# First mLSTM layer of a two-layer decoder step: values with tokens on partitions, stabiliser rows spread by DMA, sample queries in four column groups

## The chip, the cores and the metric

One core of one Trainium2 chip runs the whole program. The metric is the device time of one execution in microseconds. The kernel before took 1507.76 us, the median of three runs (1506.08 to 1508.02). The execution that the profiler recorded took 1506.18 us; its trace spans 1504.4 us, and all times "at" below are microseconds from the start of that span.

## The reference

A prompt of 512 tokens and 8 single-token samples, 520 columns in all, pass through two layers of width 1024. Each layer is a token mixer, a gated MLP with a width-3 causal convolution (inner width 2816), and a per-layer embedding term. Layer 0 mixes with an mLSTM (4 heads, keys of 128, values of 256), layer 1 with sliding-window attention. The change touches layer 0's mixer alone. Written for one head over the whole prompt (zero initial state, so that the chunked form of the reference comes to one causal product):

```
b = cumsum(log_sigmoid(f));   m_t = b_t + max(0, max_{s<=t}(i_s - b_s))
p[s,t]  = (k_s . q_t) / sqrt(128) * exp(b_t - b_s + i_s - m_t)      for s <= t
num_t   = sum_s p[s,t] v_s;   qn_t = sum_s p[s,t]
h_t     = num_t / max(|qn_t|, exp(-m_t));   y = (sigmoid(o) * h) @ w_out
C_new   = sum_s w_s k_s v_s^T;   n_new = sum_s w_s k_s              (the prompt's final state)
```

Each sample updates its own stored memory, C = w_old C + w_new k v^T (4 heads of 128x256), reads it with its query, and gets h in the same way. C, n and m of prompt and samples are outputs too.

## The kernel before

Everything is float32. Features lie on partitions and tokens on the free axis: `h`, `xH`, `xL` are [128, 8, 520]. A projection runs as three rounded products (high by high, low by high, high by low), in chunks of 128 output features. For each chunk SP loads 512 KB of weights into a slot of a three-slot ring, or for some chunks one of five extra slots (`load`, L380); ACT rounds them to `wH` (`high`, L486); DVE subtracts to get `wL` (`low`, L1275); PE multiplies (L798 to L802, in `mout` L808 to L810, where each half of 260 tokens is a unit of its own); and DVE reads the result out of PSUM, scaled (L1315). Each engine's order is the order in which it is written; semaphores alone tie the engines together. PSUM has four tiles of two banks: `tile[0]`, `tile[1]`, `sums`, `side`.

Layer 0's mixer goes through these stages:

- `kv` (13 chunks): gates, keys, values. In its first chunk DVE makes the rows `brow` (cumulated log forget gate), `mrow` (running maximum) and the samples' rows; the last sets `s_rows` (L1383). `erow` is exp(-m).
- Turning: PE transposes keys and values to tokens-on-partitions (`ktok`, `vtok`, L880, L882) and turns small rows to columns (L887 to L893): `acol` holds the exponent per key token.
- `qo` (12 chunks: 4 of queries, 8 of the output gate). Behind each of the last 8 chunks stands one sample's outer product (`sample_products`, L915) and the query of the sample before (`memory_query`, L903): four matmuls, one for each head, 8 columns of stationary `qmask` and 256 moving columns of the memory. All four write partitions 0 to 7 of `sums`, side by side on the free axis. The memories go through a two-buffer ring that POOL loads and stores.
- Behind `qo`: the last query, the samples' normaliser product (L929), a copy `stok` of the queries' results (8 x 1024, L1463), eight small transposes (L933), and the samples' output (L1466 to L1479).
- Four heads. `spread_scores(n)` spreads `mrow` to 128 partitions with a 4-row matmul into `sums[:, 0]` (L942), then makes the four causal blocks of scores (L949) in `tile`. DVE adds the causal mask (`diag`, L1488, into `cg`), ACT makes the decays in `prob` (7 exponentials, L580 and L583), DVE multiplies scores in (`weights`, L1502). `values(n)` multiplies with the values as stationary, features out, up to 512 tokens moving (L964, into both banks of `side`), a column sum by a one-hot stationary of 4 columns (L966, into `tile[1][0:4, 1]`), and the final memory (L974) with its normaliser (L977, one moving column) into `sums[:, 1]`. DVE multiplies by the gate (L1526), copies the final memory (L1529), and weighs the next head's keys (`final_weights`, L1513, into `kw`).
- Behind all heads: DVE makes one over the denominators of all heads on 4 partitions (L1535 to L1538), PE spreads it by four 4-row matmuls (L992), DVE multiplies (L1549), ACT rounds to `xH` (L589), DVE makes `xL` (L1543).
- `mout` (8 chunks, 16 units), whose first unit waits for `xL` row block by row block. Loads 3 to 7 use extra slots that lie over the mixer's tensors and so wait for them (L372 to L380).

## Time and profile before

| | us |
|---|---|
| median of three runs | 1507.76 |
| the profiled execution, its own time | 1506.18 |
| its span | 1504.4 |
| PE busy (matmul) | 1431.6 |
| DVE busy | 880.7 |
| ACT busy | 571.2 |

The profile is one execution. "PEclk" in it is the clock that TensorE was granted as a share of full speed: 1.00 is the 2.4 GHz level, 0.50 the 1.2 GHz level. A PE row counts records; a float32 matmul leaves two of them, a float32 transpose one. In a timeline row the first number is where the group starts and the second how long until its last result is out; consecutive PE rows overlap, so the pace is read from the starts. In the chain of waits a piece's length is the time that it alone held the end back.

### The profile page before, as it was taken

To read this page: it belongs to the slowest core of one execution; us is meant where nothing else is said; L and a number is where in the kernel's file an instruction comes from. 1 tells how busy PE (TensorE), PEld (TensorE's weight loads), DVE (VectorE), ACT (ScalarE), POOL (GpSimd) and SP (SyncE) were. 2 spreads that over 40 slices of the span, in tenths; PEclk is the share of its full clock that TensorE was granted. 3 is DMA by queue.
4 is the path that set the end of the run, shared out by engine and by line. 5 is a ranking of instruction groups with operands and counts; after the bars stand their busy time and mean duration, and the time that the engine had idled before them with its cause. 6 is when DMAs were issued, how large, how long until landed. Compare 5 with 4: busy or idle time off the path is not lost.

```text
span 1504.4 us, 25607 instructions
## 1 busy us (share of the span) xinstructions
PE 1431.6 (95%) x11049; PEld 1352.4 (90%) x11049; DVE 880.7 (59%) x1571; ACT 571.2 (38%) x1001; POOL 32.3 (2%) x55
## 2 busy tenths in 40 slices
PE   6999989899999999999999978899999999999987
PEld 6989855699999999999889966699999999999977
DVE  4435553658777777322766565757877777522464
ACT  5121131355444444222543124655444444322452
POOL 2000100000000000000100010000000000000000
PEclk9999999899999999999999987999999999999999
DMA  7222530221223233322323230022223233322222
GB/s 224 73 83 71 185 124 0 71 85 43 76 94 94 90 96 104 117 80 90 127 71 93 76 90 1 1 88 68 71 87 97 87 96 92 124 97 86 72 57 100
DMA packets 33442, 130.86 MB, mean 87 GB/s; under 512 B 4057, under 2 KB 4145, under 8 KB 32929
## 3 DMA queue, kind: packets, MB, share of 16 engines
q1 hardware_dynamic: 28368, 110.36, 23.3%
q0 software_dynamic: 4960, 18.86, 4.0%
q8 instruction: 87, 1.43, 0.4%
q14 instruction: 27, 0.21, 0.0%
HBM read 120.57 MB, written 10.04 MB: 87 GB/s over the span
## 4 chain that ended last, share of the span: by engine, by line
PE 86%; DVE 9%; ACT 3%; issue 1%; DMA 1%; SPq 0%; POOL 0%; DVEq 0%; ACTq 0%
PE tile L798 21%; PE tile L800 21%; PE tile L802 21%; PE tile L808 3%; PE tile L809 3%; PE tile L810 3%; PE side L964 1%; PE side L1195 1%; PE sums L839 1%; DVE wL L1275 1%; DVE sm L1799 1%; DVE soft L1814 1%; ACT wH L486 1%; PE sums L903 1%; PE tile L966 1%
## 5 line engine op out<-in xcount | busy, mean ns | idle before, releaser
L486 ACT ACTIVATE wH<-raw 128x1024 fp32r<-128x1024 f32 (+1 forms) x193 | 214.3, 1111 | 487.0 <-DMA raw<-in_w_up 147.5
L798 PE MATMUL tile<-xH,wH 128*128 128x260 f32 x1872 | 381.3, 285 | 17.2 <-DVE xL L1347 11.1
L802 PE MATMUL tile<-xH,wL 128*128 128x260 f32 x1872 | 378.7, 284 | 0.0
L800 PE MATMUL tile<-xL,wH 128*128 128x260 f32 x1872 | 378.4, 284 | 0.0
L1275 DVE TENSOR_TENSOR wL<-raw,wH 128x1024 fp32r<-128x1024 f32 (+1 forms) x193 | 249.2, 1291 | 183.9 <-ACT wH L486 179.6
L798 PEld LDWEIGHTS tile<-xH,wH 128*128 128x128 f32 x1872 | 290.7, 190 | 21.2 <-issue 20.4
L802 PEld LDWEIGHTS tile<-xH,wL 128*128 128x128 f32 x1872 | 290.2, 189 | 0.0
L800 PEld LDWEIGHTS tile<-xL,wH 128*128 128x128 f32 x1872 | 289.7, 189 | 0.0
L1315 DVE TENSOR_TENSOR u<-tile,rstd 128x520 f32<-128x520 f32 x102 | 71.3, 699 | 155.1 <-PE tile L802 155.1
L798 PE MATMUL tile<-hidH,wH 128*128 128x260 f32 x616 | 124.3, 283 | 0.0
L802 PE MATMUL tile<-hidH,wL 128*128 128x260 f32 x616 | 123.8, 282 | 0.0
L800 PE MATMUL tile<-hidL,wH 128*128 128x260 f32 x616 | 123.8, 282 | 0.0
L808 PE MATMUL tile<-xH,wH 128*128 128x260 f32 x384 | 117.5, 306 | 3.3 <-DVE wL L1275 3.0
L809 PE MATMUL tile<-xL,wH 128*128 128x260 f32 x384 | 111.4, 290 | 0.0
L810 PE MATMUL tile<-xH,wL 128*128 128x260 f32 x384 | 111.2, 289 | 0.0
L800 PEld LDWEIGHTS tile<-hidL,wH 128*128 128x128 f32 x616 | 95.1, 188 | 0.0
L802 PEld LDWEIGHTS tile<-hidH,wL 128*128 128x128 f32 x616 | 94.9, 188 | 0.0
L798 PEld LDWEIGHTS tile<-hidH,wH 128*128 128x128 f32 x616 | 94.8, 188 | 0.0
L808 PEld LDWEIGHTS tile<-xH,wH 128*128 128x128 f32 x384 | 75.2, 196 | 7.3 <-DVE wL L1275 3.8
L809 PEld LDWEIGHTS tile<-xL,wH 128*128 128x128 f32 x384 | 75.2, 196 | 0.8
L810 PEld LDWEIGHTS tile<-xH,wL 128*128 128x128 f32 x384 | 75.2, 196 | 0.0
L1315 DVE TENSOR_TENSOR kvq<-tile,rstd 128x520 f32<-128x520 f32 x24 | 16.8, 698 | 81.6 <-PE tile L802 81.6
(297 smaller groups left out, 1983.3 us busy)
## 6 DMA issues: line engine op xcount, KB each, us to landing
raw<-in_w_up SPq DMA_DIRECT2D x88, 512.0 KB, 3.6
raw<-in_w_down SPq DMA_DIRECT2D x32, 704.0 KB, 4.1
raw<-in_w_ple SPq DMA_DIRECT2D x16, 512.0 KB, 3.6
raw<-in_w_kv SPq DMA_DIRECT2D x13, 512.0 KB, 3.7
raw<-in_w_qo SPq DMA_DIRECT2D x12, 512.0 KB, 3.6
raw<-in_w_qkv SPq DMA_DIRECT2D x12, 512.0 KB, 3.7
cring<-in_c_in POOLq DMA_DIRECT2D x8, 512.0 KB, 3.9
out_c_s<-cring POOLq DMA_DIRECT2D x8, 512.0 KB, 3.5
```

Of the source, the lines that this page charges most:

```text
L486: nc.scalar.activation(wH[j][:, 0:n], raw[j][:, 0:n], ACT.Copy).then_inc(s_high, 1)
L798: nc.tensor.matmul(out[:, q, 0:HT], wh, x[0][:, k, tokens(q)], start=first, stop=False)
L800: nc.tensor.matmul(out[:, q, 0:HT], wh, x[1][:, k, tokens(q)], start=False, stop=False)
L802: mm = nc.tensor.matmul(out[:, q, 0:HT], wl, x[0][:, k, tokens(q)], start=False, stop=last)
L808: nc.tensor.matmul(out, wh, x[0][:, k, tokens(q)], start=first, stop=False)
L809: nc.tensor.matmul(out, wh, x[1][:, k, tokens(q)], start=False, stop=False)
L810: return nc.tensor.matmul(out, wl, x[0][:, k, tokens(q)], start=False, stop=last)
L839: nc.tensor.matmul(sums[:, q, 0:HT], ones, sq[:, k % 2, tokens(q)], start=(k == 0), stop=(k == KT - 1)).then_inc(s_squ, 1)
L903: mm = nc.tensor.matmul(sums[0:DEC, n // 2, (n % 2) * DV:(n % 2 + 1) * DV], qmask[:, b % 2, n, :], cring[:, b % 2, n, :], start=b == 0 and ...
L964: nc.tensor.matmul(side[:, half, j * P:SEQ], vtok[:, j, n, half * P:half * P + P], pj, start=(j == 0), stop=(j == NB - 1), skip_group_chec ...
L1275: nc.vector.tensor_tensor(wL[j][:, 0:n], raw[j][:, 0:n], wH[j][:, 0:n].bitcast(F32), ALU.subtract).then_inc(s_low, 1)
L1315: nc.vector.tensor_tensor(halves(dst), bank(stage, c)[0:rows, :, 0:HT], halves(rstd[0:rows, :]), ALU.mult).then_inc(s_read, 1)
```

## The change

- Values: the stationary operand is now a 128x128 block of `prob` and the moving one the values with a 257th column of ones, so numerator and denominator come out together, tokens on partitions. For each head there are four accumulation groups (blocks 3, 2, 1, 0 with 4, 3, 2, 1 matmuls) and a fifth for the final memory (4 matmuls). The five groups go through three PSUM banks in turn.
- DVE makes one over each block's denominator (three instructions on one column, `denominators`), ACT copies the block scaled by it to `ytok` (`numerators`), PE transposes eight blocks per head back (`turn_numerators`), and DVE multiplies by the gate (`gated`). Rounding for `mout` (`x_high`, `o_low`) follows head by head. The stages behind all heads (L1535 to L1538, L992, L1549) go.
- `mrow` is stored to DRAM and read back by four DMAs, each to all 128 partitions; they are on POOL's queue, ahead of the samples' memories. The spreading matmuls (L942) go. `diag` and the decays of heads 0 and 1 are made during `qo`.
- `exp(-m)` becomes a column too: four more small matmuls and one small copy.
- A sample query's four matmuls write four partition groups, 0, 32, 64 and 96, of one bank. `stok` becomes 104 x 256, turned by two transposes.
- Order: `scores(0)` stands ahead of the last query, `scores(1)` behind the sample turns; `weights(0)` ahead of the samples' output; `low("mout", 2)` within head 1.
- `mout` loads 3 to 7 get other extra slots and other waits.

```diff
+            pool.wait_ge(s_rows, 1)
+            pool.dma_start(g.m_rows, mrow[:]).then_inc(s_mst, 16)
+            pool.wait_ge(s_mst, 16)
+            pool.wait_ge(s_squ, KT)
+            for n in range(NH):
+                pool.dma_start(mspread[n], g.m_rows[n:n + 1, :].to_broadcast([P, SEQ])).then_inc(s_mspread, 16)
...
@@ mout loads
                 if stage == "mout" and k == NRING:
-                    sp.wait_ge(s_snum, DEC)
+                    sp.wait_ge(s_st_t, 1)
                 if stage == "mout" and k == NRING + 1:
-                    sp.wait_ge(s_num, NH)
                     for b in range(2):
                         sp.wait_ge(s_cst[b], 16 * DEC // 2)
                 if stage == "mout" and k == NRING + 2:
+                    sp.wait_ge(s_num, NB * NH)
+                if stage == "mout" and k == NRING + 3:
                     sp.wait_ge(s_cps, 16)
+                if stage == "mout" and k == NRING + 4:
                     sp.wait_ge(s_afin, NH + 1)
+                    sp.wait_ge(s_out, 16 * 4)
...
@@ ACT
+            def numerators(n):
+                for i, b in enumerate(reversed(range(NB))):
+                    e = (NB + 1) * n + i
+                    act.wait_ge(s_num, NB * n + i + 1)
+                    act.wait_ge(s_den, NB * n + i + 1)
+                    nc.scalar.activation(ytok[:, b, :], num_bank(e)[:, 0:DV], ACT.Copy,
+                                         scale=rden[:, (NB * n + i) % (2 * NB):(NB * n + i) % (2 * NB) + 1]
+                                         ).then_inc(s_nr, 1)
...
             for c in range(COUNT["qo"]):
                 high(*ahead("qo", c + 2))
+                if c in (1, 5):
+                    decays(c // 4)
...
+            for n in range(NH):
+                numerators(n)
+                if n + 2 < NH:
+                    decays(n + 2)
+                x_high(n)
...
@@ PE
+                nc.tensor.matmul(sums[:, 1, 160 + NH * b:160 + NH * b + NH], erow[:, b * P:b * P + P],
+                                 ident[0:NH, 0:NH], start=True, stop=True)
...
@@ memory_query
-                    mm = nc.tensor.matmul(sums[0:DEC, n // 2, (n % 2) * DV:(n % 2 + 1) * DV], qmask[:, b % 2, n, :],
-                                          cring[:, b % 2, n, :], start=b == 0 and n % 2 == 0, stop=b == DEC - 1,
+                    mm = nc.tensor.matmul(sums[32 * n:32 * n + DEC, 0, 0:DV], qmask[:, b % 2, n, :],
+                                          cring[:, b % 2, n, :], start=b == 0, stop=b == DEC - 1,
                                           skip_group_check=True)
...
+            def num_bank_free(e):
+                n, i = divmod(e - 3, NB + 1)
+                if e == 2:
+                    pe.wait_ge(s_qnr, 1)
+                if e >= 3 and i == NB:
+                    pe.wait_ge(s_cfr, n + 1)
+                elif e >= 3:
+                    pe.wait_ge(s_nr, NB * n + i + 1)
+
             def values(n):
                 pe.wait_ge(s_prob, n + 1)
...
+                for i, b in enumerate(reversed(range(NB))):
+                    e = (NB + 1) * n + i
+                    num_bank_free(e)
+                    for j in range(b + 1):
+                        at0 = starts[j] + (b - j) * P
+                        mm = nc.tensor.matmul(num_bank(e)[:, 0:DV + 1], prob[:, n % 2, at0:at0 + P], vtok[:, j, n, :],
+                                              start=(j == 0), stop=(j == b))
+                    mm.then_inc(s_num, 1)
+                e = (NB + 1) * n + NB
+                num_bank_free(e)
+                pe.wait_ge(s_kw, n + 1)
                 for j in range(NB):
...
+                    mm = nc.tensor.matmul(num_bank(e)[:, 0:DV + 1], kw[:, j, :], vtok[:, j, n, :], start=(j == 0),
+                                          stop=(j == NB - 1))
                 mm.then_inc(s_cf, 1)
+            def turn_numerators(n):
+                pe.wait_ge(s_nr, NB * (n + 1))
+                pe.wait_ge(s_afin, n + 1)
+                for half in range(2):
+                    for b in range(NB):
+                        mm = nc.tensor.transpose(turned_num(half)[:, b * P:b * P + P],
+                                                 ytok[:, b, half * P:half * P + P], ident)
+                mm.then_inc(s_numt, 1)
+            scores(0)
+            memory_query(DEC - 1)
...
+            scores(1)
             for n in range(NH):
                 values(n)
                 if n + 2 < NH:
-                    spread_scores(n + 2)
+                    scores(n + 2)
+                turn_numerators(n)
...
@@ DVE
+            def denominators(n):
+                for i, b in enumerate(reversed(range(NB))):
+                    dve.wait_ge(s_num, NB * n + i + 1)
+                    r = rden[:, (NB * n + i) % (2 * NB):(NB * n + i) % (2 * NB) + 1]
+                    total = num_bank((NB + 1) * n + i)[:, DV:DV + 1]
+                    chain.link(nc.vector.scalar_tensor_tensor(out=r, in0=total, scalar=-1.0, in1=ecol[:, b, n:n + 1],
+                                                              op0=ALU.mult, op1=ALU.max))
+                    chain.link(nc.vector.tensor_tensor(r, total, r, ALU.max))
+                    nc.vector.reciprocal(r, r).then_inc(s_den, 1)
...
             for c in range(COUNT["qo"]):
                 scaled_read("qo", c, kvq[:, c + 3 * NH if c < NH else c, :])
                 low(*ahead("qo", c + 2))
+                if c in (0, 4):
+                    diag(c // 4)
                 if c >= NH:
                     new_memory(c - NH)
...
             for n in range(NH):
                 if n + 1 < NH:
                     weights(n + 1)
+                if n:
+                    o_low(n - 1)
+                denominators(n)
+                last_memory(n)
                 if n + 1 < NH:
                     final_weights(n + 1)
                 if n + 2 < NH:
                     diag(n + 2)
+                if n == 1:
+                    low("mout", 2)
+                gated(n)
             clear_acc()
+            o_low(NH - 1)
```

## Rows read from the trace of the kernel before

**Rows 1.** The page: shares of the span in the chain that ended last.
```profile
PE 86%; DVE 9%; ACT 3%; issue 1%; DMA 1%; SPq 0%; POOL 0%; DVEq 0%; ACTq 0%
```
**Rows 2.** Windows: stretch, length, busy us (records) by engine, PEclk, DMA share, GB/s.
```profile
204.00:223.00 19.00, 13.92 (x45) 7.01 (x44) 10.49 (x26) 10.45 (x18) 1.59 (x3) 0.84 0.26 83
223.00:271.00 48.00, 47.99 (x180) 24.79 (x179) 14.65 (x28) 4.72 (x14) 0.00 (x0) 0.99 0.04 9
271.00:289.00 18.00, 12.54 (x32) 7.31 (x33) 15.75 (x18) 5.61 (x9) 0.65 (x2) 0.62 0.19 68
```
**Rows 3.** Chain of waits around the heads: start, us, what held the end.
```profile
213.96 1.28 ACT L580
...
272.79 3.35 DVE mrow L1538
```
**Rows 4.** PE timeline of the heads and of `mout`'s second unit: start, us, what.
```profile
222.75 2.46 PE L964 MATMUL side<-prob,vtok 128*128 128x512 f32 x4
...
234.62 2.42 PE L949 MATMUL tile<-kvq 128*128 128x512 f32 x8
...
248.17 2.42 PE L949 MATMUL tile<-kvq 128*128 128x512 f32 x8
...
270.04 0.95 PE L977 MATMUL sums<-const,cv 128*128 128x1 f32 x8
...
289.10 0.28 PE L808 MATMUL tile<-xH,wH 128*128 128x260 f32 x1
```
**Rows 5.** PE timeline of one sample query, one of seven behind `qo` chunks.
```profile
195.10 1.89 PE L903 MATMUL sums<-cring,qmask 128*8 128x256 f32 x8
196.93 0.51 PE L798 MATMUL tile<-xH,wH 128*128 128x260 f32 x2
```
**Rows 6.** Layer 1: matmuls of two column halves on PE, and the clock there.
```profile
900.17 1.12 PE L1218 MATMUL sums<-softT,vst 128*64 128x128 f32 x8
...
900.10:901.25 1.15, 1.15 (x10) 0.75 (x9) 0.91 (x4) 0.38 (x1) 0.00 (x0) 0.50 0.80 175
```
**Rows 7.** PE timeline of the turning stage: transposes and rows made columns.
```profile
103.31 0.60 PE L882 MATMUL side<-const,kvq 128*128 128x128 f32 x4
103.75 0.27 PE L880 MATMUL sums<-const,kvq 128*8 128x128 f32 x1
...
113.58 1.05 PE L887 MATMUL sums<-const,cv 4*128 4x4 f32 x8
```
**Rows 8.** DVE timeline: the operations that the new order uses.
```profile
204.98 1.65 DVE L1442 SCALAR_TENSOR_TENSOR cring<-cring,sbc,side 128x256 f32<-128x256 f32 x4
...
211.84 0.19 DVE L1469 TENSOR_TENSOR rs<-rs,sbc 128x32 f32<-128x32 f32 x1
212.07 0.35 DVE L1470 RECIPROCAL rs<-rs 128x32 f32<-128x32 f32 x1
...
237.89 1.68 DVE L1502 SCALAR_TENSOR_TENSOR prob<-tile,prob 128x512 f32<-128x512 f32 x4 [2.48 <-ACT prob L580]
244.52 1.29 DVE L1526 TENSOR_TENSOR kvq<-side,kvq 128x512 f32<-128x512 f32 x2 [4.94 <-PE tile L966]
...
283.49 1.30 DVE L1543 TENSOR_TENSOR xL<-kvq,xH 128x520 fp32r<-128x520 f32 x2
```
**Rows 9.** ACT timeline: a copy out of PSUM, and two roundings to `xH`.
```profile
283.60 1.17 ACT L589 ACTIVATE xH<-kvq 128x520 fp32r<-128x520 f32 x2 [1.19 <-DVE kvq L1549]
...
289.30 0.39 ACT L528 ACTIVATE y_ml<-tile 128x260 f32<-128x260 f32 x1 [1.23 <-PE tile L810]
```
**Rows 10.** DVE timeline in `kv`: a chunk's `wL`, and the end of the chunk before.
```profile
62.82 1.23 DVE L1275 TENSOR_TENSOR wL<-raw,wH 128x1024 fp32r<-128x1024 f32 x1
67.85 0.70 DVE L1315 TENSOR_TENSOR kvq<-tile,rstd 128x520 f32<-128x520 f32 x1 [3.81 <-PE tile L802]
```
**Rows 11.** Windows of layer 1's attention: columns as in rows 2.
```profile
900.00:920.00 20.00, 15.20 (x85) 11.68 (x83) 8.73 (x29) 6.87 (x25) 0.00 (x0) 0.67 0.07 21
...
940.00:960.00 20.00, 17.51 (x138) 12.81 (x136) 14.70 (x43) 12.58 (x48) 0.00 (x0) 1.00 0.00 1
```

More of the change, by code:

```diff
@@ L100 @@
 STACK = 64 + DEC
+STOK = 32 * (NH - 1) + DEC
 class Chain:
@@ L475, in o_tile, with num_bank, turned_num @@
             return kvq[:, NH + k, :]
+        def num_bank(e):
+            return (tile[1][:, 1, :], side[:, 0, :], sums[:, 1, :])[e % 3]
+        def turned_num(half):
+            return (side[:, 1, :], sums[:, 0, :])[half]
         @block.scalar
@@ L959, in values @@
-                at0 = 0
-                for j in range(NB):
-                    w = SEQ - j * P
-                    pj = prob[:, n % 2, at0:at0 + w]
-                    for half in range(2):
-                        nc.tensor.matmul(side[:, half, j * P:SEQ], vtok[:, j, n, half * P:half * P + P], pj,
-                                         start=(j == 0), stop=(j == NB - 1), skip_group_check=True)
-                    mm = nc.tensor.matmul(tile[1][0:NH, 1, j * P:SEQ], hot[:, n, :], pj, start=(n == 0 and j == 0),
-                                          stop=(n == NH - 1 and j == NB - 1), skip_group_check=True)
-                    at0 += w
@@ L979, in values @@
-                mm.then_inc(s_cf, 1)
-            spread_scores(0)
-            spread_scores(1)
+                starts = [j * SEQ - j * (j - 1) // 2 * P for j in range(NB)]
+                for i, b in enumerate(reversed(range(NB))):
[6 more added lines that the diff above has]
+                    mm.then_inc(s_num, 1)
@@ new lines, in _ @@
+            scores(0)
+            memory_query(DEC - 1)
+            pe.wait_ge(s_prod, 1)
+            nc.tensor.matmul(sums[:, 1, 0:NH * DEC], ones, ntmp[:, 0].rearrange("p n b -> p (n b)"),
+                             start=True, stop=True).then_inc(s_qns, 1)
+            pe.wait_ge(s_stok, 1)
+            for half in range(2):
+                mm = nc.tensor.transpose(side[:, 1, half * P:half * P + STOK], stok[:, half * P:half * P + P],
+                                         ident[0:STOK, 0:STOK])
@@ new lines, in last_memory, with gated, o_low @@
+            def last_memory(n):
+                dve.wait_ge(s_cf, n + 1)
+                nc.vector.tensor_copy(cfin[:, n, :], num_bank((NB + 1) * n + NB)[:, 0:DV + 1]).then_inc(s_cfr, 1)
+            def gated(n):
+                dve.wait_ge(s_numt, n + 1)
+                for half in range(2):
+                    o = kvq[:, NH + 2 * n + half, 0:SEQ]
+                    last = nc.vector.tensor_tensor(o, turned_num(half), o, ALU.mult)
+                last.then_inc(s_afin, 1)
+            def o_low(n):
+                for k in (2 * n, 2 * n + 1):
+                    dve.wait_ge(s_xh, XSET["mout"] + k + 1)
+                    nc.vector.tensor_tensor(xL[:, k, :], o_tile(k), xH[:, k, :].bitcast(F32), ALU.subtract
+                                            ).then_inc(s_xr, 1)
@@ new lines, in _ @@
+            mask(0)
+            for c in range(COUNT["qo"]):
+                scaled_read("qo", c, kvq[:, c + 3 * NH if c < NH else c, :])
+                low(*ahead("qo", c + 2))
+                if c in (0, 4):
+                    diag(c // 4)
+                if c >= NH:
+                    new_memory(c - NH)
+            wold, wnew = sbc[:, :, 0, :], sbc[:, :, 1, :]
+            chain.did(nc.vector.tensor_tensor(nst[:], nst[:], wold, ALU.mult))
+            chain.link(nc.vector.tensor_tensor(ntmp[:, 0], kvq[:, 0:NH, SEQ:T], wnew, ALU.mult))
@@ new lines, in _ @@
+            dve.wait_ge(s_qnr, 1)
+            chain.link(nc.vector.scalar_tensor_tensor(out=flat_rs, in0=flat_rs, scalar=-1.0, in1=flat_rs,
+                                                      op0=ALU.mult, op1=ALU.max))
+            chain.link(nc.vector.tensor_tensor(rs[:], rs[:], sbc[:, :, 2, :], ALU.max))
+            chain.link(nc.vector.reciprocal(rs[:], rs[:]))
+            dve.wait_ge(s_st_t, 1)
+            for half in range(2):
+                chain.did(nc.vector.tensor_tensor(
+                    stmp[:, :, half, :],
+                    side[:, 1, half * P:half * P + P].rearrange("p (n x) -> p n x", n=NH)[:, :, 0:DEC],
+                    rs[:], ALU.mult))
```

191 lines of the change are left out of this document (63 added, 128 removed).

## The prediction

> **What bounds the kernel now.** I read first the shares of the chain of waits: PE holds 86% of the span and DVE 9% [rows 1], so time is won where PE does less or stands still less. Then the windows around the mixer's core [rows 2]. Three stretches differ. From 204 to 223 PE is busy 13.9 of 19 us at a granted clock of 0.84. From 223 to 271, the four heads, it is busy without a gap at 0.99, while DVE works 15 and ACT 5 of 48 us. From 271 to 289 it is busy 12.5 of 18 us at 0.62. So the heads are bound by PE's own work and the two ends by short serial steps on other engines, with a clock that falls to its 1.2 GHz level behind them. The chain shows such steps: 1.28 us of ACT ahead of the first exponential (its table) and 3.35 us of DVE for one reciprocal over 512 columns on 4 partitions [rows 3]. One head with scores behind it takes 248.17 - 234.62 = 13.55 us; the heads last from 222.75 to 270.99, 48.2 us, and `mout`'s second unit starts at 289.10, 18.1 us later [rows 4].
>
> **Part 1, rows made columns: +1.0 us.** Four more matmuls like L887, which took 1.05 us for four [rows 7], in a stretch where PE runs without waiting. Their DVE copy lies in DVE's idle time.
>
> **Part 2, queries in four column groups: -7.1 us ahead of the last memory.** A query takes 196.93 - 195.10 = 1.83 us of PE [rows 5], about 0.22 for each of eight records. Nothing of before runs four groups of 32 columns; the nearest is layer 1's L1218, whose outputs lie in two halves of 64 partitions. Eight records of 128 columns took at most 1.12 us at a clock of 0.50 [rows 6]. One after the other they would take 8 x 0.22 = 1.76 us: transposes of 128 columns come every (103.75 - 103.31)/4 = 0.11 us at full clock [rows 7], so 0.22 at half. Two halves do run side by side. For four groups the best is 2 records in sequence, 0.45 us, the worst the 1.83 of now, or 0.1 more if each group has an entry of its own. I take 0.65, near the best, since two halves came close to halving. That saves 1.2 us for each of the six queries that stand wholly before the last sample's update; the other two are counted in part 3.
>
> The Trainium skill, "TensorE: Matmul & The Clock Gate", Part 3 (packing small matmuls), has three column tiles 2.38 times as fast as one by one. By that a query would cost 1.83/2.38 = 0.77 us, an estimate, and the part would save 0.7 us less. The rows on two halves show side-by-side work, not how far four go.
>
> **Part 3, from the last memory to the first values: -10.5 us.** Before, DVE ends the last memory at 204.98 + 1.65 = 206.6 [rows 8] and values start at 222.75 [rows 4]: 16.1 us, in which the samples' output, spreading, mask, table load, exponentials and scores stand in line. In the new order masks and decays of heads 0 and 1 are made during `qo` and `scores(0)` runs while DVE updates the last memory. Left is: last query 0.65; DVE's four small operations, begun with the query, end at 0.8 (0.2 each); `weights(0)` 1.6 [rows 8] to 2.4; `stok` 0.4 (256 columns against 0.65 for 512, L1526) to 2.8; PE's two transposes and the hop 0.4; `scores(1)` 2.4 [rows 4] to 5.6. The samples' output lies beside `scores(1)`. 16.1 - 5.6 = 10.5. The masks in `qo` add 0.7 us to DVE and the decays 2.4 us to ACT (DVE's wait between mask and weights, L1502 in rows 8), in chunks of 5.8 us or more where both idle; without that cover the sum of 3 us would come back for each head.
>
> **Part 4, four heads: 48.2 to 38 us, -10.2.** PE's work is 14 matmuls of 257 columns at 1.83/4 = 0.46 [rows 5], 6.4 us; scores 2.4 for the first two heads; eight transposes at 0.11, 0.9 with their entry. That is 9.6 or 7.3 us, if nothing waits. But PE's fourth group needs the bank of the first, and the fifth that of the second; each bank is freed by three DVE steps and an ACT copy. The nearest rows for the DVE steps are 0.19 (whose successor starts 0.23 later) and 0.35 for a reciprocal of 32 columns [rows 8]; I take 0.55 for three on one column, with 0.9 as the upper bound and 0.4 as the lower, and 0.4 for the copy (0.39, L528) [rows 9]. Counted from the first values:
> - Head 0: DVE is free in time. 9.6.
> - Head 1: mask 2 ends at about 8.2, ACT loads its table (1.3) [rows 3] and makes decays (2.4): 11.9. `weights(2)` 1.6, `o_low` 1.3 (L1543) [rows 8], one turnover 0.95: 15.8. PE could have started the fourth group at 13.7: 2.1 us lost. End 21.3.
> - Head 2: `gated(1)` 1.3 (L1526), `weights(3)` 1.6, `o_low` 1.3, turnover 0.95 with hops: 26.6; the fourth group could start at 25.4: 1.2 lost. No scores. End 29.8.
> - Head 3: no `weights`; about 0.3 lost. End 37.4; with hops between engines 38.
> `low("mout", 2)` (1.23) lies in head 1 while PE makes scores and transposes. The two DVE operations and the copy of the final memory that stand before the mask, at most 0.65 each, fit beside the scores.
>
> **Part 5, behind the heads: 18.1 to 3.8 us, -14.3.** One over all denominators, its spreading and four multiplications are gone, and `xL` for heads 0 to 2 is ready. PE goes straight into the first unit with six of eight row blocks. The last two wait for `gated(3)` 1.4, ACT's two roundings 1.17 [rows 9], the second `o_low` 0.65, and one block of products 0.4: 3.7, or 3.8 with hops. The moved loads have cover: load 5 now waits for the last numerators, 6 for the stored memory, 7 for `gated(3)`, and with some 2.9 us for a unit their chunks come later than 4 us of landing and 2.3 of rounding.
>
> **Part 6, spreading by DMA: 0.** 1 MB into SBUF around 45 to 60 us, beside weight loads. A chunk's `wL` was done at 64.05 and needed at 67.85 [rows 10]: 3.8 us of slack. Bounds 0 and +3 (a load held up by twice its slack, once). Nothing on POOL's queue is due before the first memory is stored, some 90 us later.
>
> **The clock: +4.** The new heads stall at 1 to 2 us, three times, and the start has two idle stretches near 2 us. Layer 1's attention has such alternation: 0.67 granted while PE was busy 15.2 of 20 us, but 1.00 at 17.5 of 20 [rows 11]. I price 8 us of PE work at the 1.2 GHz level, which adds 4; the bounds are 0 and about 9 (all 32 us of PE work in the heads at 0.7, less the stalls that this fills).
>
> **Sum.** 1.0 - 7.1 - 10.5 - 10.2 - 14.3 + 4 = -37.1 us. The profiled execution took 1506.18 (span 1504.4), so 1469.1; the median is 1.6 above it: 1470.7, which I put at 1470.5.
>
> **The rivals.**
> - *The clock falls through the heads.* Waits for freed banks break PE's work up as in layer 1's slow stretch [rows 11], against it stands its fast stretch with much the same work. Price: +9 instead of +4, 1475.5. The Trainium skill, "TensorE: Matmul & The Clock Gate", "A second HAM failure mode: psum-queue depth-cycling", says that going round PSUM banks can make small idles after which the clock swings between its levels. By that rule this is the case that comes; layer 1 shows both.
> - *The column groups don't run side by side.* Then the part does nothing of what it says: 8 x 1.2 = 9.4 back, 1480. For it: no row has 32-column groups; against it L1218 [rows 6].
> - *The turnover of banks is dearer.* 0.9 for DVE's three steps holds the fourth and fifth group back by 0.35 each in three heads, 2.1 us; with the DMA's 3 us, 1475.6.
> - *Slower than before.* The clock stays at 1.2 GHz from the start of the heads on. Each microsecond of PE work at full clock costs one more; stalls absorb 4. It decides at 41 + 4 = 45 us of such work: all of the heads (32) and the first five of `mout`'s 16 units. If all units ran so: 32 - 4 + 46 = 74 more than the 1466.5 without a clock term, 1541. Against it: behind the stall before `mout` the clock came back within the first unit, at 289 [rows 4], and PE has no wait behind it.
>
> **How the numbers follow.** Forecast 0.66 (its own range 1463 to 1475), clock 0.13, columns 0.10, turnover 0.06, slower 0.04, no change 0.01. The time is the forecast's, 1470.5. Downwards the range takes in no clock loss (-4), a query at 0.45 (-1.6) and cheaper hops: 1461. Upwards it takes in the columns' case with half a clock term more: 1484. About 0.2% (3 us) is what can be told from no change. Faster 0.95, same 0.01, slower 0.04.
>
> **What would show it.** In the profile after: a query near 0.65 us of PE with record starts close together; first values 5 to 6 us behind the last memory; the heads 38 us long with PE waiting for ACT's `ytok` copies ahead of each fourth group, most in head 1; L1535 to L1549 gone and `mout`'s second unit within 4 us of the last transposes; no longer idle time of ACT on loads from 45 to 65 us. I am wrong if the heads take over 45 us, if a query stays at 1.8 us, or if PE waits for DVE at the first mask.

## The result, and the profile after

| | before | after |
|---|---|---|
| median, us | 1507.50 (1506.08 to 1508.02, 4 runs) | 1465.34 (1459.84 to 1466.75, 4 runs) |
| profiled execution, its own time | 1506.18 | 1466.03 |
| its span | 1504.4 | 1464.2 |
| PE busy / DVE busy / ACT busy | 1431.6 / 880.7 / 571.2 | 1395.0 / 876.8 / 579.0 |

The ratio is 0.9718, with a 95% interval of 0.9701 to 0.9736: 42.2 us less between the medians, 40.2 between the spans. The point was 1470.5, so it lay 5 us too high; the time is inside the range of 1461 to 1484.

The first view is the chain of waits of the kernel after, by engine. It answers to [rows 1].

```profile
PE 85%; DVE 10%; ACT 2%; issue 2%; DMA 1%; SPq 0%; POOL 0%; DVEq 0%; ACTq 0%
```

The shares hardly move, since 1300 of the 1460 us are the same work. The windows say more. These three of the kernel after run from the last memory to the first values, over the four heads, and to `mout`'s second unit. They answer to [rows 2], with the columns of those.

```profile
199.30:205.40 6.10, 4.46 (x21) 2.71 (x22) 4.49 (x18) 1.85 (x2) 1.59 (x3) 0.83 0.54 171
205.40:242.30 36.90, 33.70 (x162) 27.24 (x161) 24.90 (x82) 17.10 (x37) 0.00 (x0) 0.98 0.08 26
242.30:246.40 4.10, 3.47 (x28) 3.08 (x26) 3.46 (x6) 2.11 (x3) 0.55 (x1) 1.00 0.42 163
```

Before, the same three took 16.1, 48.2 and 18.1 us [rows 2, 4]. PE is now busy 33.7 of the heads' 36.9 us, where it was busy all of 48, and DVE and ACT carry 24.9 and 17.1 instead of 15 and 5. The granted clock over the heads is 0.98.

The PE timeline of the kernel after shows the heads; it answers to [rows 4]. A row is start, length, line, operands, records, and the idle time in front.

```profile
161.30 0.62 PE L945 MATMUL sums<-cring,qmask 128*8 128x256 f32 x8
...
202.21 3.37 PE L980 MATMUL tile<-kvq 128*128 128x512 f32 x8
205.37 2.59 PE L1002 MATMUL tile<-vtok,prob 128*128 128x257 f32 x8
...
215.34 1.90 PE L1002 MATMUL sums<-vtok,prob 128*128 128x257 f32 x8
...
220.72 0.70 PE L1002 MATMUL sums<-vtok,prob 128*128 128x257 f32 x2 [1.31 <-ACT ytok L606]
...
226.03 1.90 PE L1002 MATMUL side<-vtok,prob 128*128 128x257 f32 x8
...
231.40 0.70 PE L1002 MATMUL side<-vtok,prob 128*128 128x257 f32 x2 [1.31 <-ACT ytok L606]
...
234.56 1.90 PE L1002 MATMUL tile<-vtok,prob 128*128 128x257 f32 x8
...
239.20 0.70 PE L1002 MATMUL tile<-vtok,prob 128*128 128x257 f32 x2 [0.58 <-ACT ytok L606]
...
242.28 0.37 PE L848 MATMUL tile<-xH,wH 128*128 128x260 f32 x1
...
245.31 0.39 PE L848 MATMUL tile<-xH,wH 128*128 128x260 f32 x1 [0.63 <-DVE xL L1552]
...
246.38 0.28 PE L848 MATMUL tile<-xH,wH 128*128 128x260 f32 x1
```

The four rows of eight records (205.37, 215.34, 226.03, 234.56) are the first groups of the heads, so the heads take 9.97, 10.69, 8.53 and 7.72 us. The rows of two records with an idle time are each head's fourth group, waiting for the copy that frees the first group's bank. The chain of waits through head 1 (start, us, what held the end) tells why that copy is late:

```profile
215.57 0.57 issue
216.15 0.68 DVE kvq L1546
216.83 1.59 DVE prob L1514 x4
218.42 1.22 DVE xL L1552 x2
219.74 0.17 DVE rden L1535
219.93 0.17 DVE rden L1536
220.19 0.48 ACT ytok L606
220.72 0.70 PE sums L1002 x2
```

DVE makes the second half of `gated(0)`, `weights(2)` and `o_low(0)`, 3.5 us of the path in a line, before it comes to the denominator for which ACT and then PE wait. `weights(2)` and `o_low(0)` are the sequence that part 4 of the forecast named; `gated(0)` it had off the path in head 1.

**The ledger.** All times are read from the two PE timelines and the DVE timelines.

| step | forecast | measured | from |
|---|---|---|---|
| 1, rows made columns | +1.0 | +0.9 | from start to start: eight matmuls in 1.88 us, 113.23 to 115.11, where four took 0.98 before, 113.58 to 114.56 |
| 2, six queries | -7.1 | -7.8 | 1.30 less for each, by e1 to e3 |
| 3, last memory to first values | -10.5 | -10.1 | 6.04 for 16.1 |
| 4, heads | -10.2 | -11.3 | 36.9 for 48.2 |
| 5, behind the heads | -14.3 | -14.0 | 4.1 for 18.1 |
| 6, DMA | 0 | 0 | chunks of `kv` every 5.77 us in both |
| clock | +4 | within 3 and 4, and behind the mixer | below |

The sum to `mout`'s second unit is 289.10 - 246.38 = 42.7 us less; the parts give 42.3. From there to the end the code is the same, and it took 1215.3 us before and 1217.8 after: 2.5 us go back.

### The profile page after: what moved, and what is told of

Read it like the earlier page. It is cut to its first block, busy times and chain, and to the rows that moved or that the text cites. A ratio compares the mean times of both kernels' runs of the same rounds, so it can differ in the third digit from the quotient of the medians.

```text
span 1464.2 us, 25626 instructions
## 1 busy us (share of the span) xinstructions
PE 1395.0 (95%) x11019; PEld 1345.6 (92%) x11019; DVE 876.8 (60%) x1613; ACT 579.0 (40%) x1017; POOL 35.3 (2%) x61
## 4 chain that ended last, share of the span: by engine, by line
PE 85%; DVE 10%; ACT 2%; issue 2%; DMA 1%; SPq 0%; POOL 0%; DVEq 0%; ACTq 0%
PE tile L838 22%; PE tile L842 22%; PE tile L840 22%; PE tile L848 3%; PE tile L849 3%; PE tile L850 3%; PE side L1241 1%; PE sums L879 1%; DVE sm L1852 1%; DVE wL L1321 1%; DVE soft L1867 1%; DVE cv L1346 1%; ACT wH L507 1%; PE side L848 1%; PE side L850 1%
## 5 line engine op out<-in xcount | busy, mean ns | idle before, releaser
L838 PE MATMUL tile<-xH,wH 128*128 128x260 f32 x1872 | 380.9, 285 | 16.7 <-DVE xL L1393 10.4
```

What stands on the lines that cost most here:

```text
L838: nc.tensor.matmul(out[:, q, 0:HT], wh, x[0][:, k, tokens(q)], start=first, stop=False)
```

## The experiments

All but e1 and e11 are edits of the kernel after. Landmarks are us from the start of each profiled span: the end of the last sample memory, the first values, `mout`'s first product and second unit, the span, and what is left from the second unit to the end. They were read from the timelines.

| kernel | median | memory | values | `mout` | 2nd unit | span | rest |
|---|---|---|---|---|---|---|---|
| before | 1507.50 | 206.63 | 222.75 | 283.35 | 289.10 | 1504.4 | 1215.3 |
| after | 1465.34 | 199.33 | 205.37 | 242.28 | 246.38 | 1464.2 | 1217.8 |
| e1 groups only | 1495.94 | 197.24 | 214.30 | 274.32 | 279.85 | 1494.2 | 1214.3 |
| e2 one group | 1473.16 | 208.12 | 215.07 | 251.30 | 255.40 | 1471.4 | 1216.0 |
| e3 two groups | 1469.01 | 202.75 | 209.71 | 246.07 | 250.17 | 1466.6 | 1216.4 |
| e4 late masks | 1473.45 | 201.10 | 213.51 | 250.12 | 254.23 | 1471.6 | 1217.4 |
| e5 `o_low` late | 1459.50 | 200.22 | 206.70 | 240.07 | 244.17 | 1457.6 | 1213.4 |
| e6 no denominators | 1460.88 | 198.77 | 205.51 | 237.51 | 241.62 | 1459.3 | 1217.7 |
| e7 rounding behind | 1465.63 | 199.64 | 206.38 | 242.30 | 247.21 | 1463.1 | 1215.9 |
| e8 spread twice | 1467.89 | 201.90 | 208.65 | 244.87 | 248.99 | 1466.5 | 1217.5 |
| e9 best | 1457.83 | 199.22 | 203.97 | 237.07 | 240.87 | 1455.9 | 1215.0 |
| e10 after again | 1465.91 | 200.55 | 206.89 | 243.49 | 247.59 | 1465.0 | 1217.4 |
| e11 table ahead | 1503.05 | 208.45 | 225.51 | 285.52 | 291.06 | 1505.3 | 1214.2 |

The rest varies between 1213.4 and 1217.8 us though its code is the same. The end of the last memory varies too, from 198.77 to 200.55 in the kernels whose code up to there is that of after (e5, e6, e7, e9, e10). So small differences are read from one landmark to the next, and not from one column. The kernel before, run beside them, took 1506.63, 1504.78 and 1506.16 us in the three groups of runs (e1 to e4, e5 to e8, e9 to e11).

### e1, e2, e3: the column groups

e1 is the kernel before with the queries in four column groups and nothing else:

```diff
-                    mm = nc.tensor.matmul(sums[0:DEC, n // 2, (n % 2) * DV:(n % 2 + 1) * DV], qmask[:, b % 2, n, :],
-                                          cring[:, b % 2, n, :], start=b == 0 and n % 2 == 0, stop=b == DEC - 1,
+                    mm = nc.tensor.matmul(sums[32 * n:32 * n + DEC, 0, 0:DV], qmask[:, b % 2, n, :],
+                                          cring[:, b % 2, n, :], start=b == 0, stop=b == DEC - 1,
```

> The kernel before with one part of the change alone: sample queries in four column groups, stok as 104 x 256, two transposes. Theory (four groups run side by side): a query falls from 1.83 to 0.55 us of PE, the six chunks behind which a query stands come every 6.95 instead of 8.27 us (-7.9), the last query gives 1.3, the stok copy 0.7 and the transposes 0.2: about -10 us, 1497.4. Rival 1 (this gain depends on the rest of the change, or the clock behind it eats it): less than -5. Rival 2 (groups don't overlap): 1507.

Ratio 0.9938 (0.9916 to 0.9960): 10.7 us less by the medians. e2 is the reverse, the kernel after with the lines marked "-" above put back (`stok` is 8 x 1024 again, turned by eight transposes, and one small product moved to another bank):

> The changed kernel with the queries put back into one group (partitions 0 to 7, heads side by side in two banks), stok 8 x 1024, eight transposes; the normaliser product goes to the bank of the first values. Theory: six queries give back 1.3 us each (+7.9), the last two and the longer stok copy about +2: +10 us, 1475. Rival (in the changed kernel another engine holds the chunks back, so that PE's query time is partly hidden): under +5.

Ratio 0.9782 (0.9759 to 0.9804): 7.8 us more than after, where 10 were expected; `mout`'s second unit comes 9.0 us later, and the rest is 1.8 shorter. e3 puts heads 0 and 1 at partitions 0 and 64 of one bank, heads 2 and 3 at the same partitions of the other (with four transposes for `stok`, and the small product moved as in e2):

```diff
-                    mm = nc.tensor.matmul(sums[32 * n:32 * n + DEC, 0, 0:DV], qmask[:, b % 2, n, :],
+                    at0 = 64 * (n % 2)
+                    mm = nc.tensor.matmul(sums[at0:at0 + DEC, n // 2, 0:DV], qmask[:, b % 2, n, :],
```

> The changed kernel with the queries in two groups, partitions 0 and 64, heads taking turns. Theory (time is set by how many records stand in line in one group, 0.216 us each, beside an entry of 0.1): a query takes about 0.97 instead of 0.55 us, +2.5 us over six queries and +0.5 in stok and its transposes: +3, 1468.5. Rival (two groups already take all there is to take): equal to the changed kernel. Rival (the entry of each group costs, not the records): a query cheaper than 0.55.

Ratio 0.9758 (0.9738 to 0.9779): 3.7 us more than after. One sample query in the PE timelines of e1, of e2 and of e3:

```profile
152.24 0.62 PE L904 MATMUL sums<-cring,qmask 128*8 128x256 f32 x8
```

```profile
155.25 1.89 PE L945 MATMUL sums<-cring,qmask 128*8 128x256 f32 x8
```

```profile
155.15 1.04 PE L946 MATMUL sums<-cring,qmask 128*8 128x256 f32 x8
```

The distance from one query to the next, a `qo` chunk in between, is 6.97 us in e1, 8.27 in e2, 7.41 in e3, 6.97 in after and 8.27 in before. So a query costs PE 1.83 us in one group, 0.97 in two and 0.53 in four. The pace of the queries comes from the groups alone, with and without the rest of the change, and the rival that they don't run side by side falls.

### e4: masks and decays of heads 0 and 1 behind `qo`

```diff
-                if c in (0, 4):
-                    diag(c // 4)
...
+            diag(0)
             weights(0)
...
+            diag(1)
             final_weights(0)
```

ACT's `decays(0)` and `decays(1)` go behind `qo` likewise.

> The changed kernel with masks and decays of heads 0 and 1 made behind qo instead of beside it. Theory (part 3 of the prediction: their cover is worth it): mask 0.7 and seven exponentials 2.1 with the table load 1.3 stand behind the sigmoid and the last mout rounding: weights(0) ends near 206 instead of 201.6, first values near 210 instead of 205.4: +4.7 us, 1470. Rival (something else, such as the samples' output, ends that stretch anyway): within 1 us of the changed kernel.

Ratio 0.9780 (0.9760 to 0.9801): 8.1 us more than after. From the last memory to the first values it is 12.4 us instead of 6.0. The PE timeline of e4 there:

```profile
208.80 0.61 PE L1029 MATMUL side<-const,stok 104*128 104x104 f32 x2 [6.58 <-DVE stok L1570]
209.20 4.51 PE L980 MATMUL tile<-kvq 128*128 128x512 f32 x8
```

PE idles 6.58 us for `stok`, which stands behind `weights(0)` on DVE, and that behind the decays: 5.1 more than the 1.51 of after. `scores(1)` then runs at the 1.2 GHz level throughout, which is the rest. So the cover in `qo` is worth 6.4 us in part 3's 10.1, 1.7 more than was expected ahead of this run; the prediction had put it at 3 us for each of the two heads.

### e5, e6: what holds the heads

e5 changes the order on DVE in each head:

```diff
-                if n:
-                    o_low(n - 1)
                 denominators(n)
+                if n:
+                    o_low(n - 1)
```

> The changed kernel with o_low(n-1) moved from ahead of denominators(n) to behind it, on DVE alone. In the changed kernel's trace PE waits 1.3, 1.3 and 0.6 us ahead of the fourth group of heads 1, 2 and 3, for ACT's copy, which waits for DVE, which is making xL. Theory (the bank turnover is late because DVE is busy, not because its chain is long): these waits go, heads 36.9 to 33.7 us, about 1462. Rival (the chain of three DVE steps and a copy, about 1.1 us, is itself what PE waits for): under 1 us gained. Rival (o_low then delays the last copies and the gate): gain given back behind the heads.

Ratio 0.9700 (0.9674 to 0.9726). The heads take 33.4 us instead of 36.9; 3.1 of the 3.5 us are in heads 1 to 3, the other 0.4 in head 0, which ran for less time at the lower clock. The fourth group of head 1, on e5's PE timeline, follows without a wait; in after it waited 1.31 us:

```profile
219.27 1.03 PE L1002 MATMUL side<-vtok,prob 128*128 128x257 f32 x4
220.40 0.70 PE L1002 MATMUL sums<-vtok,prob 128*128 128x257 f32 x2
```

What is left of the gap is some 0.25 us (groups of 4 records start 0.87 ahead of the next where PE doesn't wait, here 1.13). e6 leaves out the division of the prompt's outputs by the denominators: DVE's small steps go, and ACT copies each block as it is and doesn't wait for DVE.

```diff
-                    act.wait_ge(s_den, NB * n + i + 1)
-                    nc.scalar.activation(ytok[:, b, :], num_bank(e)[:, 0:DV], ACT.Copy,
-                                         scale=rden[:, (NB * n + i) % (2 * NB):(NB * n + i) % (2 * NB) + 1]
-                                         ).then_inc(s_nr, 1)
+                    nc.scalar.activation(ytok[:, b, :], num_bank(e)[:, 0:DV], ACT.Copy).then_inc(s_nr, 1)
```

> The changed kernel with the division left out: ACT copies the numerators unscaled and waits for PE alone, and DVE's twelve one-column operations for each head go (the prompt's outputs are then not divided). Theory: the turnover waits go as in the other kernel, -3.2 us, and nothing more, since PE then is the bound of a head: 1462. Rival (PE waits for PSUM banks or for its own mode changes, whoever reads): the waits of 1.3 us stay. Rival (DVE's time is a bound of its own): heads under 33 us.

Ratio 0.9704 (0.9675 to 0.9733). The heads take 9.1, 9.1, 6.9 and 6.9 us, 32.0 in all. That is PE's own work with nothing in the way. In heads 1 to 3 after has 4.0 us above it, and e5's order takes 3.1 of them. So most of the cost of the three small DVE steps was not their length (0.16 us each, 0.19 apart) but what stood before them; 0.9 us remain with the division in e5's order.

### e7: rounding for `mout` behind all heads

```diff
-                x_high(n)
+            for n in range(NH):
+                x_high(n)
```

and DVE's `o_low` likewise, behind the last head.

> The changed kernel with x_high and o_low of all heads behind the last head, so that the overlap of part 5 is undone for heads 0 to 2. Theory: the heads gain the 3.2 us that o_low held up the turnover, and mout's first unit then waits for eight o_low in a row (4.9 us behind clear_acc), 3.2 us later: the sum is 0 to +3, 1465 to 1468, the upper end if the clock falls in that wait. Rival (the overlap is worth what the prediction books for it, with no price in the heads): +5 or more.

Ratio 0.9734 (0.9707 to 0.9762): the same time as after. The PE timeline of e7 shows what the head by head rounding is for:

```profile
239.13 0.60 PE L1019 MATMUL sums<-const,ytok 128*128 128x128 f32 x4
242.30 0.36 PE L849 MATMUL tile<-xH,wH 128*128 128x260 f32 x1 [2.58 <-DVE xL L1553]
...
244.02 0.42 PE L851 MATMUL tile<-xH,wL 128*128 128x260 f32 x1
...
247.21 0.28 PE L849 MATMUL tile<-xH,wH 128*128 128x260 f32 x1
```

The last transposes start 2.8 us earlier than in after (239.13 against 241.92), the heads being free of `o_low`. Then PE waits 2.58 us for `xL`, and from about 243.4 to 246.6 its products take 0.42 us instead of 0.28, the 1.2 GHz level. From the first values to the last transposes it is 32.75 us (after 36.55), from there to the second unit 8.08 (after 4.46): 3.8 won, 3.6 lost. Of the 3.8, 0.7 is head 0, which e7 ran in 9.28 us and after in 9.97. So the rounding within the heads is worth 3.6 us of part 5's 14.0, and in the order of after it costs part 4 the 3.1 us that e7 wins in heads 1 to 3. The order of e5 keeps the 3.6 (4.46 us from the last transposes to the second unit, as in after) and has the 3.1 too. The other 10.4 us of part 5 are the stages that went (L1535 to L1538, L992, L1549 before); no run puts them back one by one.

### e8: the spreading DMAs twice

```diff
+            pool.wait_ge(s_mspread, 16 * NH)
+            for n in range(NH):
+                pool.dma_start(mspread[n], g.m_rows[n:n + 1, :].to_broadcast([P, SEQ])).then_inc(s_mspread, 16)
```

DVE then waits for both sets ahead of its first mask.

> The changed kernel with the four spreading DMAs issued twice, one set after the other: 1 MB more beside the weight loads of kv. Theory (part 6: slack hides them): 0, 1465; ACT's waits for two kv loads grow by one or two us and DVE's and PE's do not. Rival (they do delay a chunk): +1 to +3 us in the stretch from 45 to 75 us.

Ratio 0.9739 (0.9704 to 0.9773). POOL issues the first set from 43.87 to 46.03 us in after, and the two sets from 44.80 to 46.95 and from 50.84 to 52.96 in e8. ACT's timelines in `kv` show the weight loads on both sides of that time: first of after, then of e8.

```profile
43.42 1.06 ACT L507 ACTIVATE wH<-raw 128x1024 fp32r<-128x1024 f32 x1 [6.37 <-DMA raw<-in_w_kv]
53.91 1.06 ACT L507 ACTIVATE wH<-raw 128x1024 fp32r<-128x1024 f32 x1 [9.43 <-DMA raw<-in_w_kv]
```

```profile
44.32 1.06 ACT L510 ACTIVATE wH<-raw 128x1024 fp32r<-128x1024 f32 x1 [6.22 <-DMA raw<-in_w_kv]
57.04 1.06 ACT L510 ACTIVATE wH<-raw 128x1024 fp32r<-128x1024 f32 x1 [11.66 <-DMA raw<-in_w_kv]
```

ACT waited 9.43 us for the second load in after (9.30 before) and 11.66 in e8, so with the second set it came about 2.2 us later. Still nine chunks took 51.90 us there (DVE's reads of them, 51.27 to 103.17) as in after (50.21 to 102.11). The slack of [rows 10] took even the doubled transfer, and part 6 at nothing holds. The medians of e8 and after differ by 2.5 us, and their intervals overlap. In the profiles the last memory ends 2.6 us later in e8, and neither part of that needs the second set. 1.05 us is there at a read of DVE's early in `kv` (41.62 against 40.57), ahead of the DMAs; e10, the kernel after once more, has this read at 41.83. The other 1.5 us come at one place. These windows (columns of [rows 2]) start at the same chunk, first in after and then in e8:

```profile
112.11:122.11 10.00, 10.00 (x73) 9.76 (x74) 5.95 (x14) 2.10 (x4) 0.00 (x0) 0.83 0.01 2
113.17:123.17 10.00, 10.00 (x60) 9.75 (x61) 4.32 (x12) 2.10 (x4) 0.00 (x0) 0.66 0.01 2
```

PE is busy throughout in both; at a granted clock of 0.66 it gets 13 records less done than at 0.83. e3, e4, e6 and e7 have the longer stretch at the 1.2 GHz level there too, without a second set.

### e11: part 3's head load apart from the rest

e11 is the kernel before with one more instruction, which makes ACT load its table for the exponential while it waits:

```diff
             high("mout", 2)
+            nc.scalar.activation(touch[:], eps[:], ACT.Exp)
             for n in range(NH):
```

> The kernel before with one small Exp of a constant put on ACT behind the last rounding ahead of the heads, so that the table is loaded while ACT waits for the first mask. Theory (in before the load of 1.28 us stands on the path between mask 0 and decays 0; in the changed kernel it ran ahead of the wait, which is why head 1 came 1 us shorter than forecast): first values 1.2 to 1.3 us earlier behind the last memory, 14.8 instead of 16.1 us. Rival (the load is hidden or moves back behind the wait): 16.1.

Ratio 0.9981 (0.9969 to 0.9993). The ACT timeline of e11, then its DVE and PE timelines in one stretch:

```profile
210.29 1.28 ACT L572 ACT_TABLE_LOAD   x1
...
216.14 0.40 ACT L581 ACTIVATE prob<-cg,acol 128x128 f32<-128x128 f32 x1 [4.36 <-DVE cg L1489]
```

```profile
219.99 1.68 DVE L1503 SCALAR_TENSOR_TENSOR prob<-tile,prob 128x512 f32<-128x512 f32 x4 [3.94 <-PE tile L950]
```

```profile
215.25 4.63 PE L950 MATMUL tile<-kvq 128*128 128x512 f32 x8
```

The load did leave the path: the first exponential starts with the mask, and the decays are done at 218.5. But `weights(0)` then waited for `scores(0)`, which ran at the 1.2 GHz level (4.63 us, against 2.42 at full clock). From the last memory to the first values this execution took 17.1 us, not the 14.8 hoped for. In the kernel before, `scores(0)` took 4.10 us and ended at 217.18, and the decays at 217.61: only 0.4 us apart, so taking 1.28 us off the decays could give 0.4 there and no more. By the medians the timed runs are 3.1 us shorter, with an interval that ends just below 1. But the profile is of the slowest of the ten (1507.14; the others took 1501.69 to 1505.63), so it doesn't show where that comes from, and the effect of the table load alone stays open. What e11 does show is that in the order of before the slow scores lie just behind the decays, so that in this execution they took the place of the load. The change takes the load, the mask and `scores(0)` off the path at once.

### e9, e10: a better version, and after once more

e9 is after with e5's order, with ACT rounding each half of a head as soon as it is gated, and with `scores(1)` ahead of the sample transposes:

```diff
-                act.wait_ge(s_afin, n + 2)
                 for k in (2 * n, 2 * n + 1):
+                    act.wait_ge(s_afin, 1)
+                    act.wait_ge(s_gated_half, k + 1)
...
+            scores(1)
             pe.wait_ge(s_stok, 1)
...
             mm.then_inc(s_st_t, 1)
-            scores(1)
```

> The changed kernel with three moves that the runs so far point to: o_low(n-1) behind denominators(n) (as in the earlier run, -3.3 us); ACT rounds each half of a head as soon as its half is gated, instead of when both are (-0.6 us ahead of the last two row blocks of mout's first unit); scores(1) ahead of the two sample transposes, so that PE begins it when weights(0) is done and not when stok is (-0.4). Theory: about 1 us under the earlier run in first values to mout's second unit, 4.3 under the changed kernel; 1459 by the same clock. Rival (the sample chain or DVE then ends those stretches): no more than the -3.3 of the first move.

Ratio 0.9690 (0.9667 to 0.9713): 8.1 us less than after beside it (e10). From the last memory to the second unit it is 41.65 us, against 47.05 in after and 43.95 in e5. First values come 4.75 us behind the last memory, since `scores(1)` no longer waits for `stok`. The PE timeline of e9:

```profile
201.53 2.42 PE L981 MATMUL tile<-kvq 128*128 128x512 f32 x8 [1.18 <-DVE prob L1516]
```

Here it is at full clock (2.42 us), where in after it was not (3.37). So of the 1.3 us that this stretch is shorter, 0.9 is the clock's. Between the profiled spans of e9 and e10 (1455.9 and 1465.0) lie 9.1 us: 5.4 from the last memory to the second unit, 2.4 in the rest (1215.0 against 1217.4), where the code is the same, and 1.3 ahead of the last memory, where it is the same too. So 5.4 us is what the three moves, e5's among them, are shown to be worth in these executions. This is the fastest of the versions run.

e10 is the kernel after once more:

> The changed kernel once more, beside the others of this call. What is open: 42.7 us were won up to mout's second unit, but the profiled span is 40.2 shorter; from that unit to the end it took 1217.8 us against 1215.3. Theory (nothing of the change reaches there; TensorE's clock falls at other places from one execution to the next): another execution shows 1215 to 1218, with the 1.2 GHz stretches lying elsewhere. Rival (the change makes a later stage slower): 1217.8 again with the same stretches.

Ratio 0.9731 (0.9710 to 0.9751). Its rest takes 1217.4 us, like the 1217.8 of the first profile, with stretches at the lower clock at the same places: the rival that was written down, and not the theory.

## Why the prediction was right

**The bound.** The heads were PE's own work and the ends were serial steps, as read from [rows 2, 3]. After the change the heads are at 36.9 us with 32.0 of PE's work in them (e6).

**Part 1** measured 0.9 for 1.0.

**Part 2** had the right mechanism and a size a little off. A query was put at 0.65 us and measures 0.53 to 0.55, so six give 7.8 and not 7.1. The best case had been named as 0.45. The page's figure ("TensorE: Matmul & The Clock Gate" of the Trainium skill, Part 3: three column tiles 2.38 times as fast) would have given 0.77 us, an estimate; four groups here are 1.83/0.55 = 3.3 times as fast and two 1.9 times.

**Part 3** measured 10.1 for 10.5. Up to the start of `scores(1)` it took 2.9 us for 3.2, with the terms near what was taken (the samples' steps on DVE 0.18 or 0.19 long, `weights(0)` 1.68, `stok` 0.41). Then `scores(1)` held the values back for 3.16 us instead of 2.4, for the clock. e4 shows that the cover in `qo` is what the part rests on: without it 6.4 us come back.

**Part 4** measured 11.3 for 10.2, 36.9 us of heads for 38. The mechanism was right, and three sizes were off. The largest is PE's own work: 9.6 and 7.3 us a head, 33.8 in all, was forecast, and e6 has 9.1 and 6.9, 32.0 in all. A matmul was priced at 0.46 us, a quarter of a query, and takes 0.43 (eight records in 1.73 us, 215.34 to 217.07). The waits ahead of the fourth groups were forecast as 2.1, 1.2 and 0.3, and are 1.31, 1.31 and 0.58: 3.2 in sum for 3.6. And 0.7 us of the lower clock lies in head 0.

One step of head 1 failed: "ACT loads its table (1.3)" was counted behind mask 2, as the load stood in the kernel before. It ran ahead of it. ACT's timeline of before and of after:

```profile
213.96 1.28 ACT L580 ACT_TABLE_LOAD   x1 [5.51 <-DVE cg L1488]
```

```profile
211.75 1.28 ACT L593 ACT_TABLE_LOAD   x1
214.17 0.40 ACT L593 ACTIVATE prob<-cg,acol 128x128 f32<-128x128 f32 x1 [1.14 <-DVE cg L1500]
```

The mask ends at 214.13; the load was over at 213.03. The load's 1.3 us did not all come back: `weights(2)` started 11.4 us behind the first values where 11.9 was forecast, since the mask was 0.6 later and `gated(0)`, on DVE until 216.8, took the load's place. The turnover of a bank took 1.17 us from DVE's first step (219.55) to PE's start (220.72), where 0.95 was taken: the three steps 0.54 for 0.55, the copy 0.47 for 0.4, the rest between the engines. e5 and e6 show the mechanism: with DVE's other work behind the denominators, or with no denominators, the waits are gone (in e5 some 0.25 us of one is left). The rival of a dearer turnover falls, and so does the one of DMA (e8).

**Part 5** measured 14.0 for 14.3. PE goes from the last transposes (241.92) into six blocks at once and waits 0.63 us for the last two. e7 shows what the early roundings give to this: without them PE waits 2.58 us, and 3.6 us are lost.

**The clock** is the term that failed: +4 was set. From the last memory to `mout`'s second unit the only stretch at the lower level is this window of after:

```profile
203.20:206.70 3.50, 3.50 (x11) 2.56 (x10) 1.78 (x6) 0.00 (x0) 0.00 (x0) 0.52 0.85 259
```

It makes `scores(1)` 0.9 us longer (3.16 from its start to the values' start; e9 has 2.26 from its start to the next) and the first eight records of values 0.7 (2.59 for 1.90): 1.6 in all, which the ledger holds in parts 3 and 4. The heads' three waits of 1.31, 1.31 and 0.58 us cost no clock, at 0.98 granted over all heads. So 2.4 of the 4 us did not come. With the clock's 1.6 taken out, parts 1 to 5 give 43.9 us where 41.1 were forecast, most of it in part 4 (12.0 for 10.2) and part 2. 2.8 from the parts and 2.4 from the clock make the 5.2 us by which the ledger lies beyond the forecast of 37.1 at `mout`'s second unit; 2.5 are given back behind it, so part of the closeness of the point is luck. Two sums of the forecast don't come out of their terms: a head of 6.4 + 2.4 + 0.9 is 9.7 and not 9.6, and the upper bound is 1480 and half of 4, 1482 and not 1484; the lower one, 1461, leaves 3.9 us to "cheaper hops", for which it has no number. 1465.34 lies inside with or without them, since the first two downward terms alone give 1464.9.

The rival that took the clock to fall through the heads named a rule, "A second HAM failure mode: psum-queue depth-cycling" on the page "TensorE: Matmul & The Clock Gate" of the Trainium skill. The trace doesn't agree: three banks in turn with these waits kept 0.98, and what is missing is the end of the stretch above. The slower case needed the lower level in the heads and in `mout`'s first units; both ran at full clock but for the heads' first 1.4 us.

Of the signs that the prediction named, three came out a little off: the first values 6.04 us behind the last memory (5 to 6), the second unit 4.46 behind the last transposes (within 4), and head 1's wait no longer than head 2's.

**The 2.5 us given back.** These are windows of before and then of after, from `mout`'s second unit in each: 610.9 us, and the remainder.

```profile
289.10:900.00 610.90, 596.45 (x4800) 587.23 (x4798) 379.18 (x661) 242.27 (x404) 10.44 (x15) 0.99 0.28 89
900.00:1504.40 604.40, 576.33 (x4597) 553.42 (x4595) 366.34 (x701) 255.64 (x495) 3.24 (x6) 0.97 0.24 77
```

```profile
246.40:857.30 610.90, 596.94 (x4806) 587.57 (x4806) 380.17 (x664) 242.96 (x405) 10.51 (x16) 0.99 0.28 89
857.30:1464.20 606.90, 576.58 (x4592) 553.53 (x4589) 365.65 (x699) 255.15 (x494) 3.24 (x6) 0.97 0.24 76
```

The first 610.9 us hold the same work at the same clock in both. The difference is in layer 1 and behind it, with records that agree within 6 and busy times within 0.7 us, and thus idle time. The time that the rest spends at the 1.2 GHz level doesn't explain it: 51.7 us before and 52.6 in after. Nor does it order the kernels: 45.0 us in e11 with a rest of 1214.2 and 45.5 in e5 with 1213.4, but 46.6 in e8 with 1217.5 and 41.4 in e9 with 1215.0. The two profiles of the kernel after have these stretches at the same places (from 705 us in the one and 706 in the other, 838 and 839, 855 and 856, 869 and 870, 934 and 935, 1412 and 1413, 1459 and 1460), so they are no chance of one execution. Yet one timed run of after took 1459.84 us against 1464.64 to 1466.75 for the others, so some executions of it are 5 us shorter, and no profile shows where. What sets the 2.5 us stays open.

## What to carry to other kernels

Before rounding or any other work for a later stage is put on an engine, look whether an instruction that frees a bank stands behind it there: 0.5 us of division cost PE 3.2 us, because 3.5 us of other work stood ahead of it, and one exchange in the order took 3.1 back. Whoever adds up many small matmuls should read their price from starts of like ones: a quarter of another group's time made 33.8 us of 32.0 here. Matmuls with few output rows belong side by side in column groups, and the gain can be had alone. A step taken off a serial path is worth what the next latest arrival allows: masks made early were worth 6.4 us here, while for the table load by itself the wait for `scores(0)` stood 0.4 us behind it.

## What the runs showed of the hardware

- Four float32 matmuls of 128x8 against 256 columns, at partitions 0, 32, 64 and 96 of one bank, take 0.53 to 0.55 us together, two at a time 0.97, one after the other 1.83.
- ACT's table load (1.28 us) can run ahead of what its activation waits for. It ran at 211.75 in after, 2.4 us ahead of the mask's arrival, behind a copy that had just finished; before, it stood at 213.96, just behind the mask's arrival (213.88) and on the chain [rows 3]. What decides between the two was not tried.
- The idle 1.51 us ahead of the sample transposes was followed by some 3.4 us at the 1.2 GHz level in after and e10, and likewise 1.46 us in e3 and 1.52 in e5 and e6; the 0.97 us there in e2 was not, nor were the heads' three waits of up to 1.31 us in after, nor the 1.18 us ahead of `scores(1)` in e9. That these waits are the reason was not tried apart.
